# Time mixing in pairs of heads: the masked grams of the next pair formed in the tail of this one, the projections cut in six pieces between the level matmuls

## The chip, the cores and the metric

One core of a Trainium2 chip runs the whole kernel. Its engines are TensorE (PE; its weight loads are listed as PEld), VectorE (DVE), ScalarE (ACT), GpSimd (POOL) and SyncE (SP), which issues most DMAs. Each has its own queue and works through it in order; they wait for each other by semaphores. The metric is the device time of one execution in microseconds (us).

## The reference

Two transformer-like layers run on 128 context tokens and 128 latent tokens, which share the weights. All is fp32. The change touches only the time mixing of layer 0, a recurrence over the tokens in both directions, for 16 heads of 64 channels:

```python
def _rwkv7_step(S, inp):
    r, w, k, v, kk, a = inp
    sa = jnp.einsum('bdhij,bdhj->bdhi', S, -kk)
    S = S * w[..., None, :] + sa[..., None] * (kk * a)[..., None, :] + v[..., None] * k[..., None, :]
    return S, jnp.einsum('bdhij,bdhj->bdhi', S, r)
```

`r`, `k`, `v` are `(D, D)` projections of shifted inputs, `w` (decay) and `a` come from small two-step (LoRA) projections, `g` is a gate, and the result goes through a group norm per head, a bonus term `r . k . v` and an output projection. Behind it stand the SwiGLU of layer 0, the neighbourhood attention of layer 1 and its top-2 of 8 experts, which the change leaves as they are.

## The kernel before

The recurrence is solved in closed form over all 128 tokens of a sequence. The 16 heads are taken in eight pairs of two heads (`c` = 0 to 7; two heads, two sequences, so four problems `q`, and two directions `e`). Buffers of two pairs alternate (`p` = 0, 1). For each pair:

- `prep_project` (L545): r, k, v of a pair, three matmuls of eight 128-row chunks each, into PSUM banks 4 and 5. Every fp32 matmul shows as two records in the trace. `prep_gate` (L551) is the gate. ACT copies them out (`prep_rkv`, L1047 to L1053). They are made two pairs ahead (`ahead`).
- `prep_lora` (L564), `prep_norm` (L573), `prep_coef` (L579, L581), `prep_hat` (L589) prepare the next pair (`prep`): LoRA, key norms, bonus coefficients, transposes. ACT takes tanh, roots and exponentials (L1059 to L1078), DVE scans the decays (L1482) and normalises the keys (L1470, L1471), POOL forms the scaled factors (`prep_factors`, L1307 to L1319), DVE copies out bonus, v and hats (L1487, L1488, L1493).
- `gram` (L607): 128 x 128 products of those factors for each problem, twice (k = 1, 2) for each direction. DVE masks them out of PSUM (L1501) into `GB` and `GK`, and `pairs` (L1508 to L1512) starts the triangular inverse from them.
- `level_z`, `level_d` (L616, L625): five levels of doubling that grow the inverse of both 64-token halves. Each level is two blocks of eight 64 x 64 matmuls per direction; DVE masks (L1517), adds (L1526, L1524) and transposes (L1528) between them.
- `right_side` (L635, L637), `solve0`, `solve1`, `solve2` (L644, L651, L659): the solution, with a copy by ACT behind each (DVE adds the last, L1534).
- `outputs` (L673 to L685): the outputs and final state, which ACT copies out. The group norm of a pair (`gn_mean` L690, `gn_var` L694, on DVE L1539 to L1552) is done in the step of the next.

The order of all this is written out by hand: `mix_step` on each engine lists what is issued, and no planner moves it. `c` = 0 has a prologue. In PE's step the grams of the pair come first, then the LoRA of the next pair, the levels, the right side, and the three solves, each behind one of the three projections of the pair after next. The direction `e` uses PSUM banks 2e and 2e + 1 for grams, levels and solves alike.

## Time and profile before

| | us |
|---|---|
| three timed runs | 2109.75, 2120.48, 2122.73 (median 2120.48) |
| the profiled execution, its own time | 2112.75 |
| its span, first to last instruction | 2111.0 |
| time-mixing stage, first gram to output projection | 168.3 to 614.1 |
| PE, DVE, ACT, POOL busy over the whole span | 1840.9, 1400.8, 1091.5, 134.4 |

The page gives the mean granted clock of PE as 0.932 of full speed. A record of the timeline gives start and duration in us, engine, line, what it writes and reads, and how many instructions were merged; in brackets stands the idle time ahead of it and what ended that. The durations of matmuls are modelled at their end, so two records in a row overlap by a little: what one takes is best read from start to start.

### The profile page before, as it was taken

To read this page: it belongs to the slowest core of one execution; us is meant where nothing else is said; L and a number is where in the kernel's file an instruction comes from. 1 tells how busy PE (TensorE), PEld (TensorE's weight loads), DVE (VectorE), ACT (ScalarE), POOL (GpSimd) and SP (SyncE) were. 2 spreads that over 40 slices of the span, in tenths; PEclk is the share of its full clock that TensorE was granted. 3 is DMA by queue.
4 is the path that set the end of the run, shared out by engine and by line. 5 is a ranking of instruction groups with operands and counts; after the bars stand their busy time and mean duration, and the time that the engine had idled before them with its cause. 6 is when DMAs were issued, how large, how long until landed. Compare 5 with 4: busy or idle time off the path is not lost.

```text
span 2111.0 us, 32971 instructions
## 1 busy us (share of the span) xinstructions
PE 1840.9 (87%) x11460; PEld 1531.6 (73%) x11460; DVE 1400.8 (66%) x1978; ACT 1091.5 (52%) x1466; POOL 134.4 (6%) x208
## 2 busy tenths in 40 slices
PE   6657787888776999698984999999999999999997
PEld 5546666776665888577973787878787887878785
DVE  6824555444634555583215888888888898989897
ACT  6422222221112444482221877777778787878685
POOL 0022222122200000001100000000000000000000
PEclk9878889889787999899996999999999999999999
DMA  9501111101033555354422898888989897979890
GB/s 403 217 35 36 38 37 37 37 2 47 38 144 117 187 192 182 120 240 182 147 107 120 310 355 323 345 318 338 337 318 358 308 364 301 372 291 373 308 371 37
DMA packets 61371, 442.90 MB, mean 210 GB/s; under 512 B 7008, under 2 KB 8160, under 8 KB 10080
## 3 DMA queue, kind: packets, MB, share of 16 engines
q1 hardware_dynamic: 59184, 437.81, 54.2%
q10 hardware_dynamic: 1584, 2.79, 0.3%
q8 instruction: 62, 1.02, 0.2%
q0 software_dynamic: 512, 1.05, 0.1%
q14 instruction: 29, 0.24, 0.0%
HBM read 438.99 MB, written 2.62 MB: 209 GB/s over the span
## 4 chain that ended last, share of the span: by engine, by line
PE 79%; DVE 11%; issue 4%; ACT 3%; POOL 3%; DMA 1%; ACTq 0%; DVEq 0%; POOLq 0%
PE PS L768 30%; PE PS L794 16%; PE PS L492 4%; PE PS L545 4%; PE PS L837 3%; PE PS L524 3%; PE PS L927 2%; PE PS L625 2%; PE PS L947 2%; PE PS L842 1%; PE PS L504 1%; DVE W L1501 1%; PE PS L782 1%; PE PS L479 1%; DVE LO L1378 1%
## 5 line engine op out<-in xcount | busy, mean ns | idle before, releaser
L1378 DVE TENSOR_TENSOR LO<-W,HI 128x1024 fp32r<-128x1024 f32 x758 | 894.3, 1221 | 122.5 <-ACT HI L979 75.1
L979 ACT ACTIVATE HI<-W 128x1024 fp32r<-128x1024 f32 x758 | 785.8, 1062 | 156.1 <-PE PS L768 83.8
L768 PE MATMUL PS<-HI,XHI 128*128 128x512 f32 x968 | 391.2, 404 | 27.0 <-DVE XLO L1633 13.2
L768 PE MATMUL PS<-HI,XLO 128*128 128x512 f32 x968 | 379.2, 392 | 0.0
L768 PE MATMUL PS<-LO,XHI 128*128 128x512 f32 x968 | 292.9, 391 | 1.3 <-DVE LO L1378 0.6
L768 PEld LDWEIGHTS PS<-HI,XHI 128*128 128x128 f32 x968 | 182.3, 188 | 66.3 <-ACT HI L979 17.9
L768 PEld LDWEIGHTS PS<-LO,XHI 128*128 128x128 f32 x968 | 180.8, 188 | 45.8 <-DVE LO L1378 6.3
L768 PEld LDWEIGHTS PS<-HI,XLO 128*128 128x128 f32 x968 | 182.7, 189 | 34.9
L794 PE MATMUL PS<-HI,HHI 128*128 128x512 f32 x484 | 189.4, 391 | 1.5 <-ACT HHI L1161 1.5
L794 PE MATMUL PS<-HI,HLO 128*128 128x512 f32 x484 | 188.5, 389 | 0.0
L794 PE MATMUL PS<-LO,HHI 128*128 128x512 f32 x484 | 145.5, 389 | 0.0
L625 PE MATMUL PS<-W 64*64 64x64 f32 x1280 | 66.7, 279 | 52.9 <-DVE W L1517 52.8
L1161 ACT ACTIVATE HHI<-PS 128x256 fp32r<-128x256 f32 (+1 forms) x110 | 44.6, 406 | 120.8 <-PE PS L782 120.8
L1083 ACT ACTIVATE W<-PS 128x128 f32<-128x128 f32 x32 | 7.1, 274 | 193.2 <-PE PS L637 193.2
L794 PEld LDWEIGHTS PS<-HI,HHI 128*128 128x128 f32 x484 | 90.9, 188 | 20.2 <-ACT HHI L1161 1.7
L794 PEld LDWEIGHTS PS<-LO,HHI 128*128 128x128 f32 x484 | 90.9, 188 | 19.1
L794 PEld LDWEIGHTS PS<-HI,HLO 128*128 128x128 f32 x484 | 90.9, 188 | 18.6
L625 PEld LDWEIGHTS PS<-W 64*64 64x64 f32 x1280 | 61.5, 189 | 57.0 <-issue 57.0
L545 PE MATMUL PS<-B,W 128*128 128x256 f32 x384 | 92.4, 398 | 3.4 <-issue 3.4
L616 PE MATMUL PS<-W 64*64 64x64 f32 x1280 | 67.0, 273 | 26.3 <-DVE W L1501 25.6
L492 PE MATMUL PS<-HI,XHI 128*128 128x512 f32 x192 | 64.7, 419 | 27.7 <-DMA CON<-cons 16.3
L545 PEld LDWEIGHTS PS<-B,W 128*128 128x128 f32 x384 | 74.5, 198 | 15.1 <-issue 3.8
(280 smaller groups left out, 2269.3 us busy)
## 6 DMA issues: line engine op xcount, KB each, us to landing
W<-w_exp SPq DMA_DIRECT2D x298, 1024.0 KB, 5.5
W<-w_mod SPq DMA_DIRECT2D x48, 1024.0 KB, 8.9
W<-w_ffn SPq DMA_DIRECT2D x33, 1024.0 KB, 4.8
W<-w_rkv SPq DMA_DIRECT2D x8, 1792.0 KB, 7.3
W<-w_qkv SPq DMA_DIRECT2D x8, 1536.0 KB, 6.8
W<-w_o SPq DMA_DIRECT2D x1, 4096.0 KB, 19.3
W<-w_o SPq DMA_DIRECT2D x1, 3072.0 KB, 9.6
W<-w_qkv SPq DMA_DIRECT2D x8, 256.0 KB, 2.8
```

Source lines behind the costliest of these rows:

```text
L492: last = mm(PS[t % 2], XHI[:, 2 * n + k, 0:P], w[:, 512 * k:512 * k + 512], start=first and k == 0, stop=end and k == 1)
L524: last = mm(PS[2 + b % 2][:, TT * half:TT * half + TT], wo_tile(l, 2 * b + half, kc), src[:, kc], start=(kc == 0), stop=(kc == C - 1))
L545: last = mm(out, w[:, n, kc], B[n][:, kc], start=(kc == 0), stop=(kc == C - 1))
L616: last = mm(PS[2 * e][h, N * q:N * q + N], GB[e][h, q, 0, h], TN[e][h, q], start=True, stop=True)
L625: last = mm(PS[2 * e + 1][h, N * q:N * q + N], left[e][h, q], right[e][h, q], start=True, stop=True)
L768: last = mm(PS[2 * (s % 2) + g], x[:, 2 * n + k, T * g:T * g + T], w[:, 512 * k:512 * k + 512], start=(n == 0 and k == 0 and i == 0 and le ...
L794: last = mm(PS[4 + 2 * g + half], h[:, f, T * g:T * g + T], w[:, 512 * half:512 * half + 512], start=(s == 0 and f == 0 and i == 0 and len ...
L837: last = mm(PS[0][:, TT * n:TT * n + TT], w[:, n, kc], HT[:, kc], start=(kc == 0), stop=(kc == C - 1))
L927: last = mm(PS[1 + 2 * (c // 4)][:, P * (c % 4):P * (c % 4) + P], HN[:, g, P * c:P * c + P], SEL[:, g], start=(g == 0), stop=(g == G - 1))
L979: fn(HI[:, u % NBUF], raw_unit(phase, u), ACT.Copy).then_inc(hi_ready, 1)
L1161: fn(HHI[:, :, 0:width], PS[2 * (s % 2)][:, 0:2 * width].rearrange("p (f t) -> p f t", f=2), ACT.Copy).then_inc(hhi_ready, 1)
L1378: tt(LO[:, u % NBUF], raw_unit(phase, u), HI[:, u % NBUF].bitcast(F32), ALU.subtract)\
```

## The change

The grams of pair c + 1 are no longer made at the start of its own step but in the tail of step c, between and behind the solves, and DVE masks them and starts the inverse there. So `GB`, `GK` and `TR` exist for two pairs; they lie in an area that the split weights of the other phases use. All grams go through banks 2 and 3, one after the other; levels, right side and solves of direction e share bank e. The projections of pair c + 2 leave the solves and go, in six pieces of four chunks, behind the `level_z` of levels 2 to 5 and behind the `level_d` of levels 4 and 5. `prep_coef` and `prep_hat` stand behind all levels. On ACT both directions' right sides are copied together. On DVE `gn_centre` stands in level 1, the key floor and the decay scan behind it, the key reciprocal behind level 2, bonus and hat behind the levels, and `gn_tail` at the end of the step. Pair 0 gets its grams in the prologue.

```diff
@@ -148,6 +148,8 @@
         CON = sb("CON", NCON)
 
 
+        with nc.sbuf_tensor("MIX", [P, 2 * NBUF * UNIT + 2 * C * TT + 4 * TT], F32) as mix_area:
+            MIX = mix_area[:, :]
         HI = sb("HI", NBUF * UNIT, F32R).rearrange("p (n x) -> p n x", n=NBUF)
         LO = sb("LO", NBUF * UNIT, F32R).rearrange("p (n x) -> p n x", n=NBUF)
         XHI = sb("XHI", C * TT, F32R).rearrange("p (c t) -> p c t", c=C)
...
@@ -223,18 +225,19 @@
         PW = two(scratch(0, 2 * TT))
         PINV, PX = CUM, CUX
         HATT = LD.rearrange("p e t -> p (e t)").rearrange("p (n t) -> p n t", n=4)
-        GB = [scratch(0, 8 * P).rearrange("p (q k t) -> p q k t", q=4, k=2) for _ in range(2)]
-        GK = [scratch(0, 8 * P).rearrange("p (q k t) -> p q k t", q=4, k=2) for _ in range(2)]
+        GB, GK = [[[MIX[:, 1024 * (4 * n + 2 * b + e):1024 * (4 * n + 2 * b + e) + 1024]
+                    .rearrange("p (q k t) -> p q k t", q=4, k=2) for e in range(2)] for b in range(2)] for n in range(2)]
         TN = [scratch(0, 4 * N).rearrange("p (q t) -> p q t", q=4) for _ in range(2)]
-        TR = [scratch(0, 4 * N).rearrange("p (q t) -> p q t", q=4) for _ in range(2)]
...
+        RHS = [RHSA[:, e] for e in range(2)]
         U = [scratch(0, 4 * N).rearrange("p (q i) -> p q i", q=4) for _ in range(2)]
         WU = RHS
...
@@ -534,25 +538,26 @@
                 return (blk[:, 0:BLK].rearrange("p (n k m) -> p n k m", n=3, k=C),
                         blk[:, BLK:BLK + 384].rearrange("p (n m) -> p n m", n=3))
 
-            def prep_project(c, r, p, n):
+            def prep_project(c, r, p, n, half):
                 w, w2 = wblock(p)
-                if n == 0:
+                if n == 0 and half == 0:
                     pe.wait_ge(pair_full[p], 16 * (r + 1))
                     if not (isinstance(c, int) and c == 0):
                         pe.wait_ge(prep_act, 4 * (c - 1) + 2)
                 out = PS[4][:, TT * n:TT * n + TT] if n < 2 else PS[5][:, 0:TT]
-                for kc in range(C):
+                for kc in range(4 * half, 4 * half + 4):
...
-                    last.then_inc(prep_psum, 1)
+                if n == 1 and half == 1:
+                    last.then_inc(rkv_psum, 1)
...
@@ -595,88 +600,95 @@
                 return slice(N * hl, N * hl + N), slice(T * g, T * g + T)
 
             def gram(e, c, p, k):
-                if k == 1:
+                use = 4 * c + 2 * (k - 1) + e
+                if use == 0:
                     pe.wait_ge(prep_pool, 3 * c + 3)
-                    if not (isinstance(c, int) and c == 0):
-                        pe.wait_ge(chain_sbuf[e], CH * c)
                 else:
-                    pe.wait_ge(gram_sbuf[e], 2 * c + 1)
+                    pe.wait_ge(gram_sbuf, use)
+                    if k == 1 and e == 0:
+                        pe.wait_ge(prep_pool, 3 * c + 3)
                 for q in range(4):
                     rows, cs = heads(q)
-                    out = PS[2 * e + q // 2][:, 256 * (q % 2):256 * (q % 2) + 256].rearrange("p (k t) -> p k t", k=2)
+                    out = PS[2 + q // 2][:, 256 * (q % 2):256 * (q % 2) + 256].rearrange("p (k t) -> p k t", k=2)
                     last = mm(out, (BT if k == 1 else KT)[p][rows, e, cs], AR[p][e][rows, :, cs], start=True, stop=True)
-                last.then_inc(gram_psum[e], 1)
-
-            def level_z(e, c, n):
+                last.then_inc(gram_psum, 1)
+
...
                 pe.wait_ge(natural_sbuf[e], 5 * c + n)
-                if n == 1:
-                    pe.wait_ge(gram_sbuf[e], 2 * c + 2)
+                if n == 1 and c:
+                    pe.wait_ge(chain_sbuf[e], CH * c)
...
-                        last = mm(PS[2 * e][h, N * q:N * q + N], GB[e][h, q, 0, h], TN[e][h, q], start=True, stop=True)
+                        last = mm(PS[e][h, N * q:N * q + N], GB[p][e][h, q, 0, h], TN[e][h, q], start=True, stop=True)
                 last.then_inc(level_psum[e], 1)
...
-                        last = mm(PS[2 * e + 1][h, N * q:N * q + N], left[e][h, q], right[e][h, q],
+                        left, right = (tr, Z[e]) if n < 5 else (Z[e], tr)
+                        last = mm(PS[e][h, 256 + N * q:256 + N * q + N], left[h, q], right[h, q], start=True, stop=True)
+                last.then_inc(level_psum[e], 1)
+
+            def right_side(c, p):
+                for e in range(2):
+                    pe.wait_ge(turned_sbuf[e], 6 * c + 6)
+                pe.wait_ge(prep_dve, 6 * c + 5)
+                for e in range(2):
+                    for q in range(4):
+                        rows, _ = heads(q)
+                        at = 2 * N * e + N * (q % 2)
+                        mm(PS[q // 2][:, at:at + N], GK[p][e][:, q, 0], VN[p][:, q % 2, rows],
+                           start=True, stop=(q % 2 == 0))
+                    for q in (1, 3):
+                        rows, cs = heads(q)
+                        at = 2 * N * e + N
+                        last = mm(PS[q // 2][:, at:at + N], AR[p][e][rows, 0, cs], S0P[p][rows, e], start=False, stop=True)
+                last.then_inc(rhs_psum, 1)
+
+            def solve0(e, c, p):
+                pe.wait_ge(rhs_sbuf, c + 1)
+                for q in range(4):
+                    for h in HALVES:
+                        last = mm(PS[e][h, 256 + N * q:256 + N * q + N], TR[p][e][h, q], RHS[e][h, q],
                                   start=True, stop=True)
...
@@ -695,36 +707,36 @@
 
             def mix_step(c, p, prep, ahead, tail):
 
-                for e in range(2):
-                    gram(e, c, p, 1)
+                if prep is not None:
+                    prep_lora(*prep)
                 if tail:
                     gn_mean(c - 1)
-                if prep is not None:
-                    prep_lora(*prep)
-                for e in range(2):
-                    gram(e, c, p, 2)
-                if tail:
-                    gn_var(c - 1)
                 if prep is not None:
                     prep_norm(prep[0])
                 for n in range(1, 6):
                     for e in range(2):
-                        level_z(e, c, n)
+                        level_z(e, c, p, n)
+                    if ahead is not None and n > 1:
+                        prep_project(*ahead, (n - 2) // 2, n % 2)
+                    if tail and n == 2:
+                        gn_var(c - 1)
                     for e in range(2):
-                        level_d(e, c, n)
-                    if prep is not None and n == 4:
-                        prep_coef(prep[0])
-                if prep is not None:
-                    prep_hat(prep[0])
-                for e in range(2):
-                    right_side(e, c, p)
-                for n, f in enumerate((solve0, solve1, solve2)):
-                    if ahead is not None:
-                        prep_project(*ahead, n)
-                    for e in range(2):
-                        f(e, c)
+                        level_d(e, c, p, n)
+                    if ahead is not None and n > 3:
+                        prep_project(*ahead, 2, n - 4)
                 if ahead is not None:
                     prep_gate(ahead[2])
+                if prep is not None:
+                    prep_coef(prep[0])
+                    prep_hat(prep[0])
+                right_side(c, p)
+                for n, f in enumerate((solve0, solve1, solve2)):
+                    if prep is not None:
+                        gram(n % 2, prep[0], prep[1], 1 + n // 2)
+                    for e in range(2):
+                        f(e, c, p)
+                if prep is not None:
+                    gram(1, prep[0], prep[1], 2)
                 outputs(c, p)
 
             modulation(0)
@@ -744,6 +756,9 @@
             prep_coef(0)
             prep_hat(0)
             prep_rkv(1, 0, 1)
+            for k in range(1, 3):
+                for e in range(2):
+                    gram(e, 0, 0, k)
             mix_step(0, 0, (1, 1), (2, 1, 0), False)
             for i in range(2):
                 mix_step(2 * i + 1, 1, (2 * i + 2, 0), (2 * i + 3, i + 1, 1), True)
...
@@ -1077,22 +1092,21 @@
                 fn(PINV, CUM, ACT.Exp, scale=-1.0)
                 fn(PX, CUX, ACT.Exp).then_inc(prep_act, 1)
 
-            def right_side(e, c):
+            def right_side(c):
+                act.wait_ge(rhs_psum, c + 1)
+                for hl in range(2):
+                    last = fn(RHSA[:, :, 2 * hl:2 * hl + 2], PS[hl][:, 0:4 * N].rearrange("p (e g i) -> p e g i", e=2, g=2),
+                              ACT.Copy)
+                last.then_inc(rhs_sbuf, 1)
+
+            def solve0(e, c):
                 act.wait_ge(chain_psum[e], CH * c + 1)
-                for hl in range(2):
-                    last = fn(RHS[e][:, 2 * hl:2 * hl + 2],
-                              PS[2 * e + hl][:, 0:2 * N].rearrange("p (q i) -> p q i", q=2), ACT.Copy)
-                last.then_inc(chain_sbuf[e], 1)
-
-            def solve0(e, c):
+                fn(U[e], PS[e][:, 4 * N:8 * N].rearrange("p (q i) -> p q i", q=4), ACT.Copy).then_inc(chain_sbuf[e], 1)
+
+            def solve1(e, c):
+                then = HALVES[1 - e]
...
@@ -1108,6 +1122,8 @@
 
             def gn_root_(c):
                 act.wait_ge(gn_psum, 3 * c + 3)
+                if not (isinstance(c, int) and c == 0):
+                    act.wait_ge(z_ready, c)
                 fn(YR, PS[7][:, 0:TT], ACT.Sqrt, scale=1.0 / N, bias=BIASES[:, 1:2]).then_inc(gn_root, 1)
 
             def mix_step(c, prep, ahead, tail):
...
@@ -1554,31 +1574,32 @@
             def mix_step(c, p, prep, tail):
                 if prep is not None:
                     prep_params(prep[0], prep[2], prep[1])
-                for e in range(2):
-                    gram(e, c, 1)
-                if tail:
-                    gn_centre(c - 1)
-                for e in range(2):
-                    pairs(e, c)
-                    gram(e, c, 2)
-                if prep is not None:
-                    prep_floor(prep[0])
-                    prep_scan(prep[0])
                 for n in range(1, 6):
                     for e in range(2):
                         level_z(e, c, n)
+                    if tail and n == 1:
+                        gn_centre(c - 1)
                     for e in range(2):
-                        level_d(e, c, n)
+                        level_d(e, c, p, n)
                     if prep is not None and n == 1:
+                        prep_floor(prep[0])
+                        prep_scan(prep[0])
+                    if prep is not None and n == 2:
                         prep_unit(prep[0])
-                    if tail and n == 2:
-                        gn_tail(c - 1, 1 - p)
-                    if prep is not None and n == 4:
-                        prep_bonus(*prep[:2])
                 if prep is not None:
+                    prep_bonus(*prep[:2])
                     prep_hat(*prep[:2])
+                    gram(0, prep[0], 1 - p, 1)
+                    gram(1, prep[0], 1 - p, 1)
+                    pairs(0, prep[0], 1 - p)
+                    gram(0, prep[0], 1 - p, 2)
                 for e in range(2):
                     solve2(e, c)
+                if prep is not None:
+                    gram(1, prep[0], 1 - p, 2)
+                    pairs(1, prep[0], 1 - p)
+                if tail:
+                    gn_tail(c - 1, 1 - p)
 
             prep_params(0, 0, 0)
             prep_floor(0)
@@ -1586,6 +1607,12 @@
             prep_unit(0)
             prep_bonus(0, 0)
             prep_hat(0, 0)
+            gram(0, 0, 0, 1)
+            gram(1, 0, 0, 1)
+            pairs(0, 0, 0)
+            gram(0, 0, 0, 2)
+            gram(1, 0, 0, 2)
+            pairs(1, 0, 0)
             mix_step(0, 0, (1, 1, 0), False)
             with dve.Fori(0, 3) as i:
                 order.enter(i, STEPS_DVE_MIX)
```

On PE at the boundary of two steps stands before (PS4 to PS7 are banks; L685 is the end of `outputs`, L607 grams, L690 the group-norm mean, L564 the LoRA):

```order
L685 MATMUL PS7<-W 64x64
L607 MATMUL PS0<-W 128x256 [waits chain_sbuf0,prep_pool]
L607 MATMUL PS0<-W 128x256
L607 MATMUL PS1<-W 128x256 x2
L607 MATMUL PS2<-W 128x256 [waits chain_sbuf1,prep_pool]
L607 MATMUL PS2<-W 128x256
L607 MATMUL PS3<-W 128x256 x2
L690 MATMUL PS7<-extra,CON 128x256 [waits gn_sbuf]
L564 MATMUL PS4<-HID,W 128x256 [waits prep_act]
```

and in the changed kernel (L697 ends `outputs`, L569 is the LoRA, L702 the group-norm mean, L578 the key norm, L622 `level_z`):

```order
L697 MATMUL PS7<-W 64x64
L569 MATMUL PS4<-HID,W 128x256 [waits prep_act]
L569 MATMUL PS5<-HID,W 128x256
L569 MATMUL PS4<-HID,W 128x256
L569 MATMUL PS5<-HID,W 128x256
L702 MATMUL PS7<-W,CON 128x256 [waits gn_sbuf]
L578 MATMUL PS6<-W,CON 128x256 [waits prep_dve,prep_pool]
L622 MATMUL PS0<-W,MIX 64x64 [waits chain_sbuf0,natural_sbuf0]
```

The grams have left this place, and the LoRA, which waits for ACT, now follows the outputs directly.

On PE inside a level stands before (level 3; L616 `level_z`, L625 `level_d`):

```order
L616 MATMUL PS2<-W 64x64 [waits natural_sbuf1]
L616 MATMUL PS2<-W 64x64 x7
L625 MATMUL PS1<-W 64x64 [waits level_mask0,turned_sbuf0]
L625 MATMUL PS1<-W 64x64 x7
L625 MATMUL PS3<-W 64x64 [waits level_mask1,turned_sbuf1]
```

and in the changed kernel (level 4; L622, L632 the same two, L549 a piece of a projection):

```order
L622 MATMUL PS1<-W,MIX 64x64 [waits natural_sbuf1]
L622 MATMUL PS1<-W,MIX 64x64 x7
L549 MATMUL PS4<-B1,W 128x256 x4
L632 MATMUL PS0<-W 64x64 [waits level_mask0,turned_sbuf0]
L632 MATMUL PS0<-W 64x64 x7
L632 MATMUL PS1<-W 64x64 [waits level_mask1,turned_sbuf1]
L632 MATMUL PS1<-W 64x64 x7
L549 MATMUL PS5<-B2,W 128x256 x4
```

Half a projection of the pair after next now stands between the blocks of a level, and in levels 4 and 5 a second half behind them.

On DVE the end of a step is before (L1493 the hat copy, L1534 the last solve's add, L1461 and L1462 the first of the next step, L1501 the gram masks):

```order
L1493 COPY W<-PS6 128x512 [waits prep_psum]
...
L1534 TENSOR_TENSOR W<-W,PS0 64x256 [waits chain_psum0]
L1534 TENSOR_TENSOR extra<-extra,PS2 64x256 [waits chain_psum1]
...
L1461 TENSOR_SCALAR W<-W 128x128 [waits gn_psum]
```

and in the changed kernel (L1518 the gram masks, L1526 to L1530 the pairs group, L1553 the last solve's add, L1565 the first of the group-norm tail):

```order
L1518 TENSOR_TENSOR MIX<-PS2,CON 128x512 [waits gram_psum]
L1518 TENSOR_TENSOR MIX<-PS3,CON 128x512
...
L1553 TENSOR_TENSOR W<-W,PS0 64x256 [waits chain_psum0]
L1553 TENSOR_TENSOR W<-W,PS1 64x256 [waits chain_psum1]
L1518 TENSOR_TENSOR MIX<-PS2,CON 128x512 [waits gram_psum]
L1518 TENSOR_TENSOR MIX<-PS3,CON 128x512
L1526 TENSOR_TENSOR W<-MIX,CON 64x256 [waits gram_sbuf]
...
L1530 STREAM_TRANSPOSE W<-W 128x256 [waits turned_sbuf1]
L1565 RECIPROCAL W<-W 128x256 [waits gn_root]
```

Masks, pairs groups and the group-norm tail now stand around the last add, in a part of the step where DVE had little queued.

## Rows read from the trace of the kernel before

**Rows 1.** Table of windows: length, busy time (count) of PE, PEld, DVE, ACT, POOL, granted clock, DMA share, GB/s
```profile
285.20:343.50 58.30, 47.81 (x570) 41.11 (x568) 30.22 (x65) 13.18 (x27) 14.86 (x22) 0.82 0.10 34
...
168.30:620.00 451.70, 359.66 (x4442) 307.88 (x4442) 234.62 (x506) 96.49 (x200) 103.88 (x154) 0.85 0.10 36
```

**Rows 2.** Timeline of PE in pair 2, first half (start, duration in us, instruction, wait)
```profile
285.24 2.10 PE L607 MATMUL PS<-W 64*128 64x256 f32 x16
...
287.90 1.13 PE L564 MATMUL PS<-HID,W 64*128 64x256 f32 x8
...
292.74 0.68 PE L616 MATMUL PS<-W 64*64 64x64 f32 x16 [0.81 <-DVE W L1501]
...
297.53 1.98 PE L625 MATMUL PS<-W 64*64 64x64 f32 x32 [0.81 <-DVE W L1517]
...
303.02 1.97 PE L625 MATMUL PS<-W 64*64 64x64 f32 x32 [1.81 <-DVE W L1517]
...
311.14 1.97 PE L625 MATMUL PS<-W 64*64 64x64 f32 x32 [4.44 <-DVE W L1517]
...
318.54 1.15 PE L625 MATMUL PS<-W 64*64 64x64 f32 x32 [0.35 <-DVE W L1517]
```

**Rows 3.** The same timeline, second half of pair 2 and start of pair 3
```profile
320.11 0.56 PE L635 MATMUL PS<-W 128*128 128x64 f32 x4
...
323.81 3.72 PE L545 MATMUL PS<-B,W 128*128 128x256 f32 x16
...
327.46 1.15 PE L644 MATMUL PS<-W 64*64 64x64 f32 x32
...
336.73 0.96 PE L659 MATMUL PS<-W 64*64 64x64 f32 x16
...
338.41 0.40 PE L673 MATMUL PS<-W 128*64 128x128 f32 x2
...
343.51 2.10 PE L607 MATMUL PS<-W 64*128 64x256 f32 x16
```

**Rows 4.** Timeline of DVE in pair 2
```profile
289.63 0.85 DVE L1508 TENSOR_TENSOR W<-W,CON 64x256 f32<-64x256 f32 x2
...
291.35 1.25 DVE L1501 TENSOR_TENSOR W<-PS,CON 128x512 f32<-128x512 f32 x2
...
300.37 1.71 DVE L1470 RECIPROCAL W<-W 128x256 f32<-128x256 f32 x1
...
305.86 1.71 DVE L1546 RECIPROCAL extra<-extra 128x256 f32<-128x256 f32 x1
...
317.34 0.39 DVE L1487 TENSOR_TENSOR W<-PS,W 128x256 f32<-128x256 f32 x1
```

**Rows 5.** Table of windows, two of 2 us in pair 2
```profile
293.20:295.20 2.00, 0.22 (x8) 0.09 (x3) 1.93 (x5) 1.58 (x2) 0.00 (x0) 1.00 0.67 136
295.20:297.20 2.00, 1.12 (x16) 0.96 (x16) 2.00 (x7) 1.35 (x2) 0.05 (x1) 0.53 0.90 373
```

**Rows 6.** Timeline of ACT and POOL in pair 2, and ACT at the start of pair 3
```profile
289.09 0.84 ACT L1059 ACTIVATE W<-PS,W 128x256 f32<-128x256 f32 x2 [1.49 <-PE PS L564]
...
293.03 1.28 ACT L1111 ACT_TABLE_LOAD   x1
...
302.62 0.73 POOL L1307 TENSOR_TENSOR W<-W 128x256 f32<-128x256 f32 x1 [4.20 <-DVE W L1471]
...
315.14 0.61 POOL L1319 TENSOR_TENSOR W<-W 128x256 f32<-128x256 f32 x1
...
345.44 0.39 ACT L1053 ACTIVATE W<-PS 128x256 f32 x1
```

**Rows 7.** Timeline of PE at the starts of pairs 6 and 7 and behind pair 7
```profile
517.40 2.10 PE L607 MATMUL PS<-W 64*128 64x256 f32 x16
...
565.17 2.10 PE L607 MATMUL PS<-W 64*128 64x256 f32 x16
...
614.14 16.11 PE L524 MATMUL PS<-HT,W 128*128 128x256 f32 x61 [4.18 <-DVE HT L1552]
```

140 lines of the change are left out of this document (63 added, 77 removed).

## The prediction

> **What bounds the kernel now.** The change touches the time-mixing stage alone, so I read first the table of windows: the stage runs from 168.3 us to about 614 us, and TensorE (PE) is busy for 360 of its 452 us, twice anything else except VectorE's (DVE) 235 [rows 1]. Next the timeline of one pair in the middle. Pair 2 starts at 285.24, when the first gram matmul (L607) issues, and pair 3 at 343.51: a period of 58.3 us [rows 2, 3], of which PE is busy for 47.8 [rows 1]. So PE bounds the stage, but not by its work alone. Its waits all stand in the first half of the pair: the first level matmuls (L616) start 7.5 us into the pair, having waited for masked grams; the level-1 product (L625) starts 12.3 us in; then 1.81 us before level 2 and 4.44 us before level 3, where DVE is in a reciprocal of 1.71 us (L1470) and later in the group-norm tail that starts with another (L1546) [rows 2, 4]. In the second half PE waits for nothing: three projections stand between the solves. Last, the clock: PE does almost nothing from 293.2 to 295.2 at a granted clock of 1.00, and at 295.2 to 297.2 the grant is 0.53, which is a mix with the 1.2 GHz level [rows 5]. From there a block of 32 level matmuls takes 1.97 us, against 1.15 once 2.4 GHz is back [rows 2].
>
> **The change, part by part.** Nothing of the arithmetic is removed. I walk one pair of the new order, with t = 0 at the end of the outputs of the pair before, durations from rows, and 0.2 us for each hand-over between engines (DVE's mask ends at 292.60, the L616 that needs it starts at 292.74) [rows 2, 4].
>
> *Start of a pair.* The grams (2.0 us each time, L607) no longer stand first; the LoRA matmuls do (L564), and they wait for ScalarE (ACT) to copy out r, k, v and gate. That copy ends at 345.44 + 0.39, 2.3 us after outputs end at 343.5 [rows 3, 6]. Before, the grams covered this; now PE idles 2.5 us, a new wait. LoRA 1.0 (its record of 1.13 overlaps the next), the group-norm mean 0.6 (2.66 us from L607 to L564, less 2.0 for the grams), the key norm about 0.5: level 1 starts at 4.7 instead of 7.5, and its product at 6.0 instead of 12.3 [rows 2], because the grams are already masked.
>
> *Levels.* At 2.4 GHz the two L616 blocks take 1.1 us, so do the two L625 blocks [rows 2], and the masks (0.4 each) and the add and transpose (0.43 and 0.45) leave about 0.9 us of waits: 3.1 us a level. A half projection is 8 of the 16 records that take 3.65 us (323.81 to 327.46) [rows 3], 1.83 us. It goes in behind the second L616, where at most 0.3 us was idle, so each piece hides little and adds about 1.5. With the group-norm variance (0.5) in level 2, the key reciprocal in front of level 3, and a second piece in levels 4 and 5 the levels come to 3.1 + 5.1 + 5.1 + 6.1 + 5.8 and 0.5 for the gate: t = 30.4.
>
> *The chain beside it.* LoRA ends at 3.5; ACT's tanh group takes 3.9 (289.09 to 293.03) [rows 6] to 7.7; DVE scans behind level 1 and 1.3 us later; ACT's group-norm root waits for the variance at 11.5, then the key root, a table load and the exponentials to 15.8; DVE's reciprocal and product (2.1) end at 16.1; GpSimd's (POOL) factors take 13.1 (302.62 to 315.14 + 0.61) [rows 6] and end at 29.4. The coefficient matmul (L579), now behind the levels, needs them: it could start at 29.5 and PE arrives at 30.4. So this chain is covered, by 0.9 us only; a delay beyond that is paid in full in every pair.
>
> *Behind the levels.* Coefficient and transposes 0.85; then PE waits 1.0 for DVE's two short operations (0.39 for the first, L1487) with their hand-overs [rows 4], which stood under level 5 before; hat 0.5; right side 3.7 (320.11 to 323.81) [rows 3]: t = 36.5.
>
> *The tail.* It was 14.6 us (323.81 to 338.41, three projections and the solves) [rows 3]. Now four gram halves of 1.0 stand there with solves of 1.1, 0.9 and 0.9. All grams use the same two banks, so each waits for DVE's mask of the one before (1.25, and in front of the third mask also the pairs group, 1.72 from 289.63 to 291.35) [rows 4]: waits of 0.4, 0.7 and 1.1. Sum 9.1, t = 45.6; outputs 5.1 (338.41 to 343.51) [rows 3]: **50.7 us a pair against 58.3**, less 7.5. The group-norm tail moves behind the last pairs group on DVE; it ends about 2 us after the outputs, under the wait of 2.5 us, and nothing of PE waits for it but LoRA's tanh, which starts later still. If it grew by over 1 us it would delay the tanh, and with it the chain to POOL.
>
> *Ends of the stage.* Pairs 1 to 5 are of this form: 5 x 7.5 = 37.5 saved. Pair 0 has its grams masked ahead of it one after the other with little to cover them: 3 lost. Pair 6 has no projections and stands on the POOL chain: 29.5 + 0.9 + 1.0 + 0.5 + 3.7 + 9.1 + 5.1 = 49.8 against 47.8 (517.40 to 565.17) [rows 7]: 2 lost. Pair 7 has no grams left, about 4 us of them and the 6 us that its levels waited for masks and DVE: 10 to 12 saved. Together 44, with PE at 2.4 GHz throughout. The chain of the whole kernel runs through the stage's end: the output projection at 614.14 waited for DVE [rows 7], so the 44 would arrive whole.
>
> *The clock.* The old pair fell to 1.2 GHz at about 295, after PE had done one block of 0.68 us since 291.93 (292.74 less its wait) [rows 2, 5]. In the new pair the emptiest place is the start, 2.5 us idle and then 2.1 of work in 2.2: somewhat busier, so I cannot say that it never falls. A fall there makes levels 1 and 2 cost 0.8 us more per pair of blocks (four of them) and less what it covers, about 3.2 us. I take it in half of the pairs: 6 x 1.6 = 10 given back. Bounds: 0, and 31 (below).
> The Trainium skill speaks of this too ("TensorE: Matmul & The Clock Gate", the section on the HAM clock gate): an idle engine is throttled to half rate and activity releases it. Taken by itself this rule says that a stage with no long idle place stays at 2.4 GHz, which would be the 44 in full; what it asks against this change is the wait of 2.5 us at each start, which no trace of the kernel before shows in that surrounding.
>
> Sum: 44 - 10 = **34 us less**. The profiled execution took 2112.75 us, its span 2111.0, and the three timed runs lie at 2109.75, 2120.48 and 2122.73; from the mean of the four, 2116, this gives **2082 us**.
>
> **The rivals.**
> (a) The clock never falls: all 44, 2072 us. For it: of the 50.7 us PE would wait in about 8. Against: the start of the pair.
> (b) The clock falls at each start and stays low until the first whole projection is through. Levels 1 to 3 (six double blocks, 0.8 each) and a projection (3.65) at half rate, less the waits that they fill: 5.2 us a pair, 31 in all; 44 - 31 = 13 less, 2103 us. For it: before, the grant stayed low from 295 to 315 through blocks that were busy most of the time.
> (c) The ACT, DVE and POOL chain ends last. It has 0.9 us of cover. Each further 1 us costs 6 to 7 us over the pairs; 2 to 4 us late gives 8 to 22, so 2090 to 2104 us. For it: scan, root and reciprocal now queue behind level 1 and 2 on DVE, and I have placed them from single rows.
> (d) The other side: the 1.2 GHz level holds through all five levels, now with the projections inside them. Then 11.0 us of projections cost 11 more, ten double blocks 0.66 each 6.6 more, less 2.7 of waits: 14.9 a pair. That is 45 slower over the kernel, 2161 us; it decides as soon as about half of the level stretch runs low. Against it: with projections between, PE has hardly a gap there.
> (e) The change does not act as written, because the dependency chain through the levels on DVE sets the pair whatever PE does: 2116 us, no change. Against it: DVE is busy 30 of 58 us [rows 1].
>
> **How the numbers follow.** Forecast 0.56, (a) 0.14, (b) 0.12, (c) 0.10, (d) 0.04, (e) 0.04. One per cent, about what a measurement here can tell, is 21 us, so the border lies at 2099. Faster by over 1%: forecast, (a), most of (c) and a little of (b), 0.79. Within 1%: the rest of (b) and (c), and (e), 0.17. Slower: (d), 0.04. The range from 2066 to 2104 takes in the forecast, (a), (c) and half of (b).
>
> **What would show it.** In the new profile: a pair period near 51 us; PE idle 2.5 us before LoRA, released by ACT; first level matmul 4.7 us and coefficient 30 us after the outputs, released by PE's own queue and not by POOL; waits of about 0.4, 0.7 and 1.1 before the later grams, released by DVE; a pair 7 near 31 us; a granted clock in the stage above 0.93 where it was 0.85 [rows 1]. Wrong, if the coefficient waits for POOL, if the grant stays low through the projections, or if DVE is what ends most level waits by more than a microsecond.

## The result and the profile after

| | before | after |
|---|---|---|
| median, us (runs) | 2116.84 (4: 2109.75 to 2122.73) | 2064.90 (4: 2063.66 to 2065.97) |
| profiled execution, its span | 2112.75, 2111.0 | 2065.11, 2063.3 |
| mean granted clock, whole span | 0.932 | 0.950 |

The ratio is 0.9756, with a 95% interval of 0.9721 to 0.9791: 2.4% faster, 52 us by the medians and 48 by the two profiles, where 34 were forecast. The median lies 1 us below the range of 2066 to 2104.

First the page of the kernel after, its span and the first and clock lines of its parts 1 and 2:

```profile
span 2063.3 us, 32930 instructions
...
PE 1820.6 (88%) x11460; PEld 1498.0 (73%) x11460; DVE 1396.7 (68%) x1978; ACT 1088.1 (53%) x1450; POOL 132.5 (6%) x208
...
PEclk9877999998988999899987999999999999999999
```

Then the windows of the kernel after: the stage, one pair without a clock fall, the start of a pair in which the clock falls, and all that stands behind the stage.

```profile
168.30:565.90 397.60, 333.22 (x4428) 269.26 (x4427) 231.27 (x508) 93.29 (x184) 101.96 (x154) 0.94 0.10 36
229.57:278.40 48.83, 42.83 (x570) 34.52 (x568) 28.29 (x62) 12.72 (x25) 14.57 (x22) 1.00 0.11 41
281.60:285.00 3.40, 3.40 (x29) 2.40 (x28) 0.05 (x1) 2.97 (x6) 0.58 (x1) 0.51 0.00 0
285.00:288.40 3.40, 2.94 (x78) 2.52 (x76) 3.11 (x9) 2.14 (x3) 0.00 (x0) 0.99 0.46 105
565.90:2063.00 1497.10, 1378.73 (x6564) 1141.66 (x6564) 1068.58 (x1319) 921.92 (x1175) 15.83 (x28) 0.97 0.69 263
```

The same stretch of the kernel before, cut at its own end of the stage:

```profile
168.30:614.10 445.80, 353.80 (x4427) 303.19 (x4426) 234.62 (x506) 96.49 (x200) 103.88 (x154) 0.85 0.09 33
```

The stage went from 445.8 to 397.6 us, by 48.2, and what stands behind it kept its length (1497.1 us; before, 614.1 to 2111.0, 1496.9). DVE's, ACT's and POOL's work is nearly the same. PE is busy 20.6 us less on the same number of matmuls, with a grant of 0.94 instead of 0.85 and a faster right side (below), and idle 27.6 us less.

One pair of the new order in the timeline of PE (pair 1; the outputs of pair 0 end at 229.65, which is t = 0; L569 LoRA, L702 group-norm mean, L622 and L632 levels, L549 projection pieces, L584 coefficients, L594 hats, L643 and L648 right side, L613 grams):

```profile
229.37 0.28 PE L697 MATMUL PS<-W 128*64 128x64 f32 x2
231.66 1.14 PE L569 MATMUL PS<-HID,W 64*128 64x256 f32 x8 [2.01 <-ACT W L1068]
232.72 0.70 PE L702 MATMUL PS<-W,CON 128*128 128x256 f32 x2
...
233.87 1.15 PE L622 MATMUL PS<-W,MIX 64*64 64x64 f32 x32
235.17 1.15 PE L632 MATMUL PS<-W 64*64 64x64 f32 x32 [0.15 <-DVE W L1535]
...
238.06 1.99 PE L549 MATMUL PS<-B,W 128*128 128x256 f32 x8
...
245.40 1.15 PE L632 MATMUL PS<-W 64*64 64x64 f32 x32 [0.39 <-DVE W L1535]
...
259.26 0.59 PE L584 MATMUL PS<-W,CON 128*128 128x256 f32 x2
...
261.05 0.66 PE L594 MATMUL PS<-CON,W 128*128 128x128 f32 x4 [0.97 <-DVE W L1505]
261.54 1.00 PE L643 MATMUL PS<-W,MIX 128*128 128x64 f32 x8
262.48 0.44 PE L648 MATMUL PS<-W 64*128 64x64 f32 x4
...
264.15 1.13 PE L613 MATMUL PS<-W 64*128 64x256 f32 x8
...
266.67 1.14 PE L613 MATMUL PS<-W 64*128 64x256 f32 x8 [0.30 <-DVE MIX L1518]
...
272.08 1.14 PE L613 MATMUL PS<-W 64*128 64x256 f32 x8 [0.84 <-DVE MIX L1518]
...
278.06 0.28 PE L697 MATMUL PS<-W 128*64 128x64 f32 x2
```

Outputs end again at 278.34: 48.7 us for the pair (49.0 from LoRA to LoRA), where the old one took 58.3 [rows 2, 3]. LoRA starts 2.0 us into the pair, level 1 at 4.2, its product at 5.5 (12.3 before [rows 2]), the coefficients at 29.6. The later gram blocks wait 0.30 to 0.84 us for DVE to mask the one before out of their banks. The levels hold no wait above 0.4 us; the old ones had 1.81 and 4.44 [rows 2].

Waits of PE by what ended them, over the stage, in the kernel before:

```profile
PE PS L625 <- DVE W L1517: 52.8, 30, 4.9
PE PS L616 <- DVE W L1501: 25.6, 16, 2.2
PE PS L579 <- POOL W L1319: 5.2, 1, 5.2
```

and in the kernel after:

```profile
PE PS L613 <- DVE MIX L1518: 15.5, 23, 1.4
PE PS L569 <- ACT W L1068: 13.2, 6, 2.3
PE PS L632 <- DVE W L1535: 7.2, 16, 2.3
PE PS L594 <- DVE W L1505: 6.7, 7, 1.0
PE PS L584 <- POOL W L1335: 4.5, 1, 4.5
```

(Columns: us in total, times, the longest.) The level products waited 52.8 us for DVE and now wait 7.2; the first level waited 25.6 us for masked grams and now waits for none. What came in their place is smaller: grams 15.5 (of it 4.2 ahead of pair 0), LoRA 13.2, hats 6.7.

### The profile page after: what moved, and what is told of

Read it like the earlier page. It is cut to its first block, busy times and chain, and to the rows that moved or that the text cites. A ratio compares the mean times of both kernels' runs of the same rounds, so it can differ in the third digit from the quotient of the medians.

```text
span 2063.3 us, 32930 instructions
## 1 busy us (share of the span) xinstructions
PE 1820.6 (88%) x11460; PEld 1498.0 (73%) x11460; DVE 1396.7 (68%) x1978; ACT 1088.1 (53%) x1450; POOL 132.5 (6%) x208
## 4 chain that ended last, share of the span: by engine, by line
PE 82%; DVE 10%; ACT 3%; issue 3%; POOL 1%; DMA 1%; ACTq 0%; DVEq 0%; POOLq 0%
PE PS L783 31%; PE PS L809 16%; PE PS L496 5%; PE PS L549 4%; PE PS L852 3%; PE PS L528 3%; PE PS L942 2%; PE PS L962 2%; PE PS L613 1%; PE PS L857 1%; PE PS L508 1%; PE PS L622 1%; DVE MIX L1518 1%; PE PS L797 1%; PE PS L632 1%
## 5 line engine op out<-in xcount | busy, mean ns | idle before, releaser
L783 PE MATMUL PS<-HI,XHI 128*128 128x512 f32 x968 | 391.2, 404 | 27.2 <-DVE XLO L1660 13.2
L809 PEld LDWEIGHTS PS<-HI,HHI 128*128 128x128 f32 x484 | 90.9, 188 | 20.2 <-ACT HHI L1178 1.7
L809 PEld LDWEIGHTS PS<-LO,HHI 128*128 128x128 f32 x484 | 90.9, 188 | 19.1
L809 PEld LDWEIGHTS PS<-HI,HLO 128*128 128x128 f32 x484 | 90.9, 188 | 18.6
L549 PE MATMUL PS<-B,W 128*128 128x256 f32 x384 | 97.2, 402 | 3.4 <-issue 3.4
L1098 ACT ACTIVATE W<-PS 128x256 f32<-128x256 f32 x16 | 5.3, 381 | 158.0 <-PE PS L648 158.0
L549 PEld LDWEIGHTS PS<-B,W 128*128 128x128 f32 x384 | 73.0, 198 | 15.5 <-issue 3.8
L1518 DVE TENSOR_TENSOR MIX<-PS,CON 128x512 f32<-128x512 f32 x64 | 40.9, 681 | 50.9 <-PE PS L613 50.9
L1641 DVE TENSOR_TENSOR HLO<-PS,HHI 128x256 fp32r<-128x256 f32 (+1 forms) x110 | 49.5, 450 | 35.2 <-ACT HHI L1178 25.1
L1431 DVE RECIPROCAL RMS<-RMS 128x256 f32<-128x256 f32 x4 | 7.0, 1753 | 95.6 <-ACT RMS L1027 95.6
```

Source lines behind the costliest of these rows:

```text
L549: last = mm(out, w[:, n, kc], B[n][:, kc], start=(kc == 0), stop=(kc == C - 1))
L783: last = mm(PS[2 * (s % 2) + g], x[:, 2 * n + k, T * g:T * g + T], w[:, 512 * k:512 * k + 512], start=(n == 0 and k == 0 and i == 0 and le ...
L809: last = mm(PS[4 + 2 * g + half], h[:, f, T * g:T * g + T], w[:, 512 * half:512 * half + 512], start=(s == 0 and f == 0 and i == 0 and len ...
L1518: last = tt(dst[:, 2 * hl:2 * hl + 2].rearrange("p q k t -> p q (k t)"), PS[2 + hl].rearrange("p (q x) -> p q x", q=2), m, ALU.mult)
L1641: tt(HLO[:, :, 0:width], PS[2 * (s % 2)][:, 0:2 * width].rearrange("p (f t) -> p f t", f=2), HHI[:, :, 0:width].bitcast(F32), ALU.subtract ...
```

## The experiments

Each is an edit of one of the two kernels. e1 to e4, e5 to e8 and e9 to e11 ran in three groups, each on another chip and each beside runs of the kernel before, whose medians there were 2112.15, 2118.05 and 2106.91; a ratio is to those runs beside it. So medians are compared within a group, and across groups the ratios.

"First gram" is where the time-mixing stage starts in the profiled execution and "stage" is the time from there to the output projection; "pairs 1 to 5" is the time from the second LoRA to the seventh, "pairs 6, 7" from there to the output projection; "low" is the time of the stage at the 1.2 GHz level, worked out from the mean granted clock of short windows. All are in us.

| run | median (runs) | ratio, 95% interval | first gram | stage | pairs 1 to 5 | pairs 6, 7 | low |
|---|---|---|---|---|---|---|---|
| before | 2116.84 (4) | | 168.3 | 445.8 | 290.4 | 94.1 | 131 |
| after | 2064.90 (4) | 0.9756, 0.9721 to 0.9791 | 168.3 | 397.6 | 249.1 | 85.1 | 49 |
| e1_before_rhs | 2104.86 (10) | 0.9970, 0.9955 to 0.9984 | 167.4 | 438.6 | 286.3 | 92.0 | 120 |
| e2_after_oldrhs | 2085.21 (4) | 0.9887, 0.9863 to 0.9910 | 165.0 | 421.0 | 259.8 | 94.9 | 85 |
| e3_before_projlevel | 2087.70 (4) | 0.9887, 0.9858 to 0.9917 | 167.6 | 430.7 | 278.5 | 95.5 | 102 |
| e4_after_projsolve | 2152.73 (4) | 1.0201, 1.0179 to 1.0223 | 168.6 | 486.0 | 322.6 | 87.2 | 178 |
| e5_filler | 2063.91 (5) | 0.9745, 0.9721 to 0.9769 | 167.7 | 400.1 | 247.3 | 89.5 | 55 |
| e6_rkv | 2065.07 (5) | 0.9747, 0.9722 to 0.9771 | 167.1 | 400.0 | 247.0 | 91.8 | 65 |
| e7_hat | 2059.88 (5) | 0.9736, 0.9712 to 0.9760 | 165.1 | 395.0 | 247.0 | 86.1 | 52 |
| e8_outorder | 2065.08 (5) | 0.9751, 0.9728 to 0.9773 | 168.2 | 398.9 | 245.8 | 90.1 | 57 |
| e9_all | 2053.85 (6) | 0.9724, 0.9694 to 0.9753 | 167.1 | 389.2 | 238.3 | 90.9 | 51 |
| e10_endfill | 2060.22 (6) | 0.9760, 0.9731 to 0.9789 | 167.0 | 397.1 | 249.1 | 84.6 | 38 |
| e11_all_endfill | 2042.18 (6) | 0.9686, 0.9655 to 0.9717 | 164.5 | 383.4 | 237.6 | 86.3 | 27 |

The first gram stands at 164.5 to 168.6 us, though PE's work ahead of it is the same in all of them. The reason is the clock ahead of the stage; here is one window of 20 us with the same work of PE, first in the kernel after, then in e7_hat:

```profile
100.00:120.00 20.00, 16.60 (x57) 13.50 (x56) 14.51 (x38) 2.44 (x4) 0.00 (x0) 0.76 0.00 1
100.00:120.00 20.00, 16.60 (x73) 14.13 (x72) 13.83 (x36) 2.43 (x4) 0.00 (x0) 0.95 0.01 1
```

So up to 4 us between two whole executions can come from ahead of the stage, and none of that belongs to an edit.

### The right side's order

I had carried the right side over at 3.7 us, and the new pair shows 2.6 (261.54 to 264.15). The diff had also regrouped its matmuls. e1_before_rhs gives the kernel before that order alone (lines that repeat `rows` and `out` are left out):

```diff
-                    mm_last = mm(out, GK[e][:, q, 0], VN[p][:, q % 2, rows], start=True, stop=(q % 2 == 0))
-                    if q % 2:
-                        mm_last = mm(out, AR[p][e][rows, 0, cs], S0P[p][rows, e], start=False, stop=True)
+                    mm(out, GK[e][:, q, 0], VN[p][:, q % 2, rows], start=True, stop=(q % 2 == 0))
+                for q in (1, 3):
...
+                    mm_last = mm(out, AR[p][e][rows, 0, cs], S0P[p][rows, e], start=False, stop=True)
```

> The kernel before, with one thing of the change: in each direction's right side all four GK matmuls are issued first and then the two of 64 rows, instead of two and one, twice. Nothing else moves. Theory (a turn between 128-row and 64-row matmuls costs time of its own, which is why a pair's right side fell from 3.7 to 2.6 us): the right side takes 2.7 us or less, the pair period falls by about 1 us, the kernel by 7 to 9 us. Rival (the right side got shorter because its operands or banks moved): 3.7 us stays, no change of the time.

Timeline of PE in e1_before_rhs, the right side of one pair (L635 the 128-row matmuls, L639 the 64-row ones, L545 the projection behind them):

```profile
317.02 1.00 PE L635 MATMUL PS<-W 128*128 128x64 f32 x8
317.96 0.44 PE L639 MATMUL PS<-W 64*128 64x64 f32 x4
318.33 1.10 PE L635 MATMUL PS<-W 128*128 128x64 f32 x8
319.36 0.44 PE L639 MATMUL PS<-W 64*128 64x64 f32 x4
...
```

The projection follows at 319.73: 2.7 us against 3.7 [rows 3], with the same matmuls. The stage is 7.3 us shorter and so are the medians, where eight right sides by 1.0 would give 8. e2_after_oldrhs is the reverse, the old order put into the new kernel (the output operand is written `...`):

```diff
                     for q in range(4):
                         last = mm(..., GK[p][e][:, q, 0], VN[p][:, q % 2, rows], start=True, stop=(q % 2 == 0))
+                        if q % 2:
+                            last = mm(..., AR[p][e][rows, 0, cs], S0P[p][rows, e], start=False, stop=True)
-                    for q in (1, 3):
-                        last = mm(..., AR[p][e][rows, 0, cs], S0P[p][rows, e], start=False, stop=True)
```

> The changed kernel with the old order inside the right side: two GK matmuls, then one of 64 rows, twice per direction; its banks, buffers and the common copy stay as changed. Theory (the order is the cause): the right side takes 3.7 us again, a pair 50.1 instead of 49.0, the kernel 7 to 9 us more than the changed one, about 2073 us. Rival (banks or buffers): 2065 us, no difference.

Timeline of PE and windows of e2_after_oldrhs:

```profile
262.19 0.66 PE L594 MATMUL PS<-CON,W 128*128 128x128 f32 x4 [0.97 <-DVE W L1504]
262.68 0.56 PE L643 MATMUL PS<-W,MIX 128*128 128x64 f32 x4
263.17 0.43 PE L646 MATMUL PS<-W 64*128 64x64 f32 x2
263.53 0.66 PE L643 MATMUL PS<-W,MIX 128*128 128x64 f32 x4
```

```profile
262.60:266.00 3.40, 3.40 (x25) 2.95 (x23) 0.69 (x1) 0.00 (x0) 0.00 (x0) 0.99 0.02 5
266.00:269.40 3.40, 3.40 (x29) 2.51 (x30) 0.79 (x2) 0.66 (x2) 0.00 (x0) 0.51 0.00 0
```

The grouped order has two turns from 128-row to 64-row matmuls and back where the old one has four, and saves 1.0 us: 0.5 for a turn there and back. The right side is back at 3.7. But the stage grew by 23.4 us, not by 8 x 1.0, and the kernel was expected 7 to 9 us longer and is 20 longer by the medians (2085.21 against 2064.90) and 28 by the ratios: 36 us more were run at the 1.2 GHz level. In the two windows PE is busy throughout, and the grant falls at the end of the slow right side; but a wait of 0.97 us, that of the hats for DVE, ends at 262.19, just ahead of them. The kernel after has the same wait there and no fall behind it. So the order is worth 7 to 8 us by itself, and in the new kernel some 15 more, by the stage, by way of the clock.

### One part of the change without the other

e3_before_projlevel leaves the grams where they were and puts the six pieces between the level matmuls; e4_after_projsolve has the grams in the tail and the projections at the solves. All else of the change (the place of the coefficients and hats, the banks, the orders of ACT and DVE, the grouped right side) is absent in e3 and present in e4:

```diff
# e3_before_projlevel, against before
                         level_z(e, c, n)
+                    if ahead is not None and n > 1:
+                        prep_project(*ahead, (n - 2) // 2, n % 2)
...
-                        prep_project(*ahead, n)
# e4_after_projsolve, against after
-                        prep_project(*ahead, (n - 2) // 2, n % 2)
...
                         gram(n % 2, prep[0], prep[1], 1 + n // 2)
+                        for half in range(2):
+                            prep_project(*ahead, n, half)
```

> The kernel before with the six projection pieces alone moved between the level matmuls; the grams stay at the start of their own pair, in four banks, and the solves stand bare. Theory (the pieces fill the waits for DVE in levels 2 and 3 and keep the clock up, which pays for most of the gain): about 20 us less than before, 2092 to 2100 us, a pair of 55 to 56 us. Rival (the gain needs the grams moved, since waits of the first level and solves without cover give all back): within 8 us of before.

> The changed kernel with the projections back between the solves, whole; the grams stay in the tail of the pair before. Theory (the coefficient matmul behind the levels then stands on the chain ACT, DVE, POOL, since the levels end some 10 us before POOL's factors, and the solves hold both projections and grams): slower than before, a pair of 60 to 62 us, 2130 to 2142 us, and PE waits for POOL 8 us or more in each pair. Rival (moving the grams is the part that gains by itself): 2090 us or less.

Waits of PE over the stage in e3_before_projlevel:

```profile
PE PS L627 <- DVE W L1521: 33.1, 18, 4.9
PE PS L618 <- DVE W L1505: 25.5, 16, 2.2
```

and in e4_after_projsolve, with the coefficient matmul of one pair:

```profile
PE PS L584 <- POOL W L1334: 35.9, 7, 5.6
PE PS L632 <- DVE W L1534: 27.1, 29, 2.3
```

```profile
337.93 1.22 PE L584 MATMUL PS<-W,CON 128*128 128x256 f32 x2 [5.10 <-POOL W L1334]
```

In e3 the pieces fill 19.7 of the 52.8 us that the level products waited, and the stage is 15.1 us shorter; the wait for masked grams is whole, 25.5. This profile is of the longest of e3's four runs (2095.15, where the others took 2082.84 to 2091.66), and by the medians e3 is 24.5 us below the kernel before, where about 20 were expected. In e4 that wait is gone, and PE reaches the coefficients about 5 us before POOL has the factors, in every pair. This is rival (c), made real by taking its cover away. The levels, short blocks with waits of DVE between them, then run low for long: 178 us of the stage against 131. So the stage is 40.2 us longer than before. The direction was expected; the wait was put at 8 us or more and the kernel at 2130 to 2142, so the low clock cost more than I had allowed for.

The parts do not add up. By the medians of this group, moving the projections into the levels is worth 24.5 us with the grams at the start (2112.15 to 2087.70), and some 88 with the grams in the tail (the stages of e4 and of the kernel after, 486.0 and 397.6). The grams in the tail, with all that moves along with them, cost 47.9 us as long as the projections stand at the solves (e1 to e4, 2104.86 to 2152.73; the stage 47.5). With the projections in the levels they save, but how much depends on the right side: with its old order 2.5 us by the medians (e3 to e2, 2087.70 to 2085.21) or 9.7 by the two profiled stages, e3's being of its longest run. With the grouped order no run holds that kernel without the grams moved. If the order were worth e1's 7.3 in e3 too, the stage of 430.7 would be 423.4, and the kernel after is 26 below that. This is an estimate; between the two, 53 us less are run at the low level.

### The start of the pair, and small edits

The longest regular waits of the kernel after are LoRA's for ACT (2.0 to 2.3 us) and the hats' for DVE (0.97). e5_filler puts four matmuls whose result nobody reads into the first; e6_rkv lets ACT copy r, k, v before the outputs; e7_hat puts the hats behind the right side; e8_outorder regroups the outputs by height, as the right side was.

```diff
# e5_filler
+                if prep is not None and tail:
+                    pe.wait_ge(prep_dve, 6 * c + 6)
+                    for k in range(4):
+                        mm(PS[6][:, TT:2 * TT], HEADS, B[0][:, k], start=True, stop=True)
                 if prep is not None:
                     prep_lora(*prep)
# e6_rkv, on ACT
-                outputs(c)
                 if ahead is not None:
                     prep_rkv(ahead)
+                outputs(c)
# e7_hat
                     prep_coef(prep[0])
+                right_side(c, p)
+                if prep is not None:
                     prep_hat(prep[0])
-                right_side(c, p)
# e8_outorder: the two S0P matmuls of q = 1 and 3 stand behind the other matmuls of all four q
```

> The changed kernel with four extra matmuls of 128 x 256 per pair (pairs 1 to 6), ahead of the LoRA, in the 2.0 to 2.3 us in which PE waits for ACT; their result is never read. They take 1.8 us, so they delay nothing. Theory (the granted clock falls at the start of a pair because PE waits there, and each fall costs 1.5 us, 50.5 against 49.0): no fall in pairs 1 to 5, all of them 49.0, 4 to 7 us less than the changed kernel, though PE does more. Rival (the difference of 1.5 us is something else, or the falls don't come from this wait): no change, or slower by what the matmuls overrun.

> The changed kernel with ACT's copy of r, k, v and gate ahead of its copy of the outputs and state, since the projections are complete long before; PE's order is as it was. Theory (the LoRA waits 2.0 to 2.3 us at the start of each pair for this copy, and that wait ends last there): the wait goes, the group-norm mean and the key norm wait some 0.5 us instead, 1.5 us less in a pair, 7 to 11 us less over the kernel. Rival (the chain ACT, DVE, POOL ends last): POOL starts earlier too, so only if PE waits for POOL at the coefficient would nothing be gained.

> The changed kernel with the four hat transposes behind the right side instead of ahead of it, so that DVE's bonus and v copies are under the right side. Theory (the wait of 0.97 us that ends with DVE's copy, L1505, is paid in full): 1.0 us less in each of pairs 0 to 6, 7 us less, and more if the denser end of the pair keeps the clock up. Rival (DVE's hat copy, which now comes later, delays the first gram mask by as much): no change, and the wait ahead of the second gram grows by 0.7 us.

> The changed kernel with the outputs' four matmuls of 64 rows at the end of the output group instead of two and two in its middle. Theory (a turn between 128-row and 64-row matmuls costs 0.15 to 0.3 us, as the right side showed): one block of them less, 0.3 to 0.5 us less in a pair, 2 to 4 us over the kernel. Rival (the shorter right side came from something special to it): no change.

Windows of e5_filler in the tail of pair 2:

```profile
308.20:311.60 3.40, 2.43 (x22) 2.10 (x21) 1.44 (x3) 0.00 (x0) 0.00 (x0) 1.00 0.01 2
311.60:315.00 3.40, 3.40 (x18) 2.67 (x17) 0.00 (x0) 0.66 (x2) 0.00 (x0) 0.51 0.00 0
315.00:318.40 3.40, 3.40 (x40) 2.98 (x40) 1.29 (x2) 0.77 (x2) 0.00 (x0) 0.50 0.02 5
```

With the start of the pair filled, no grant falls there in pairs 1 to 5 (in the kernel after it does in three of them, as at 281.6 in the window above), and the pair at full clock stays 49.0: the wait was the cause of those falls, though not each such wait brings one. But one fall came behind the hats' wait instead and lasted 6.8 us, and that pair took 51.7. Pairs 1 to 5 together are 1.8 us shorter, and pairs 6 and 7 are 4.4 us longer, with more time at the low level (31 us against 21), so that nothing is left of the 4 to 7 us that were expected. e8 goes the same way (3.3 us less, then 5.0 more), and so does e6 (2.1 less in pair 0 and 2.1 in pairs 1 to 5, then 6.7 more). Why the grant falls more often at the end of the stage in these runs is not shown.

e6 removes LoRA's wait and was expected to give 7 to 11 us. Its pair 1 takes 46.9 us, 2.1 less than 49.0, but the four pairs behind it take 49.1 to 51.6. The row of its new wait:

```profile
PE PS L578 <- POOL W L1305: 12.9, 6, 3.1
```

The longest of them, 3.1, stands in pair 0 and did so before the edit. The other five, 1.9 to 2.1 us each, are new: in pairs 2 to 6 the key norm behind LoRA waits for POOL, 9.8 us in place of the 13.2 that LoRA waited. Pair 1 alone has no such wait. e7 removes the hats' wait; every one of its pairs 1 to 5 has a fall at its start and takes 49.1 to 49.5, and its stage is the shortest of the four, 2.5 us below that of the kernel after, of an expected 7; another 3.2 us of its shorter execution lie ahead of the stage. e8 takes 0.37 us off a pair at full clock (48.65), as expected. All four ratios lie within the interval of the kernel after: none of these edits is told from it by its time.

e9_all joins the edits of e6, e7 and e8. e10_endfill fills the ends of the stage with unread matmuls, in the levels of pair 6, ahead of its coefficients, and in the waits of the last group norm; e11_all_endfill has both. (In pair 6 e10 and e11 have two `filler` matmuls in each of levels 2 to 5 and five ahead of the coefficients; the excerpt shows the end of the stage.)

```diff
+            def filler(n):
+                for _ in range(n):
+                    mm(PS[4][:, 0:TT], HEADS, CON[:, 0:TT], start=True, stop=True)
...
+            filler(1)
             gn_mean(7)
+            filler(2)
             gn_var(7)
+            filler(9)
             pe.wait_ge(z_ready, C)
```

> The changed kernel with the three edits of the runs before together: r, k, v copied ahead of the outputs, hats behind the right side, 64-row matmuls of the outputs in one block. Theory (each is worth its part in a pair at full clock: 2.1, 1.0 and 0.35 us, and what a run gives besides depends on where the granted clock falls, 1.5 us and more for each fall): undisturbed pairs of 45.5 to 46 us where they were 49.0, the stage 10 to 20 us shorter, 2045 to 2057 us. Rival (falls of the clock take back what the pairs gain, as in the runs of each edit alone): 2058 to 2066 us with more than 65 us of low grant in the stage.

> The changed kernel with extra matmuls of 128 x 256 on constants, never read, where PE waits in the last two pairs: two in each of levels 2 to 5 of pair 6 and five ahead of its coefficient matmul, which waits 4.5 us for POOL, then one, two and nine in the waits of the last group norm. Theory (in pair 6 and behind pair 7 the low grant, 20 of the stage's 50 us of it, comes from waits, and the first output projection pays for it too, 17.0 us for 64 records): the grant stays high there, PE does 12 us more work and the kernel takes 5 to 12 us less. Rival (the falls there don't come from idle time, or the extra work is in the way): no change or up to 5 us slower.

> Both together: the three edits and the extra matmuls at the end. Theory (they add up, since one acts in the pairs and the other behind them): 5 to 12 us less than the kernel with the three edits alone. Rival (the falls only move): the same time as that kernel within 3 us.

Pairs 1 and 4 of e9_all, as windows from LoRA to LoRA, both at full clock:

```profile
227.19:272.79 45.60, 42.52 (x570) 34.49 (x568) 27.86 (x61) 12.60 (x25) 14.53 (x22) 1.00 0.12 44
369.77:417.52 47.75, 42.52 (x571) 34.48 (x569) 29.45 (x66) 12.60 (x25) 14.55 (x22) 1.00 0.12 41
```

The expected 45.5 to 46 us is met by pair 1 alone. From pair 2 on the key norm waits 2.2 to 2.4 us for POOL, as in e6, and three of those four pairs take 47.75 to 48.0 without a fall. Against 49.0 that is e7's 1.0 and e8's 0.37 and no more: the wait for POOL takes e6's part back from pair 2 on.

The end of the stage in the kernel after:

```profile
565.86 17.00 PE L528 MATMUL PS<-HT,W 128*128 128x256 f32 x64 [4.18 <-DVE HT L1572]
```

and in e10_endfill:

```profile
564.10 14.08 PE L528 MATMUL PS<-HT,W 128*128 128x256 f32 x64 [0.29 <-DVE HT L1585]
```

The filler cannot shorten DVE's chain, and DVE still ends last; but the output projection starts at full clock, 14.1 us instead of 17.0 (15.7 to 17.1 in all runs without the fillers at the end, 14.08 in both with them). The profile of e10 is 4.8 us shorter by its span (2058.5): 1.3 ahead of the stage, 0.5 in it and 3.0 behind it, in this row. The fillers in pair 6 gave next to nothing in time, although 11 us less were low. The ratio of e10, 0.9760, is not told from 0.9756, and e9's 0.9724 is not either, since its interval reaches to 0.9753. e11 is at 0.9686, with an interval that ends at 0.9717, just below that of the kernel after (from 0.9721). Measured side by side, e11's median is 11.7 us below e9's and 18.0 below e10's. By the profiles of e9 and e11 that is 2.6 us ahead of the stage, which no edit made, 5.8 in it, most of that in pairs 6 and 7 (90.9 to 86.3), and 3.2 behind it; so some 8 us, within the 5 to 12 that were expected, can be the fillers'. e11 is the fastest version here: 3.1% below the kernel before; without unread matmuls it is e9, 2.8%.

## Why the prediction was wrong

The direction, the mechanism and the order of events were right; the size was not, and the median fell 1 us out of the range. By its steps, with t = 0 at the end of the outputs:

| step | forecast | measured |
|---|---|---|
| LoRA, level 1, its product start at | 2.5, 4.7, 6.0 | 2.0, 4.2, 5.5 |
| coefficients start, POOL's factors end | 30.4, 29.4 | 29.6, 28.2 |
| wait for DVE ahead of the hats | 1.0 | 0.97 |
| right side | 3.7 | 2.6 |
| tail, its waits | 9.1; 0.4, 0.7, 1.1 | 9.0; 0.30, 0.51, 0.84 |
| pair at full clock | 50.7 | 49.0 |
| pair 0; pairs 1 to 5 at full clock; pairs 6 and 7 | 3 lost; 37.5 saved; 8 to 10 saved | 2.0 lost; 45.8 saved; 9.0 saved |
| given back by the clock in pairs 1 to 5 | 8 of the 10 | 4.5 |

The last two rows are worked out from the starts of LoRA. The second one is at 229.66 before and 231.66 after, both in a stage that starts at 168.3; the next five periods sum to 290.4 and 249.1, 41.3 saved with three clock falls of 1.5 us each (periods of 50.5 instead of 49.0, and 50.2 in pair 5, which takes 48.7 without a fall in e5), so 45.8 without them; the rest of the stage is 94.1 and 85.1.

**The step that failed** is "right side 3.7", which I carried over "3.7 (320.11 to 323.81)" as unchanged work at an unchanged price. The diff in the new `right_side` put all four 128-row matmuls ahead of the two 64-row ones, and I read it as the same matmuls. It measured 2.6. e1 and e2 show what the order was worth: 1.0 to 1.1 us a pair, 7 to 9 in all, by itself, and 23 in the stage once the clock is counted in the new kernel. e2_after_oldrhs is the kernel that the prediction priced, with the right side at 3.7: it took 2085.21 (by its ratio 2093) where 2082 was forecast, well inside the range. The prediction had no row of a regrouped block, but the line of the diff should have been a term with bounds.

**The clock** was the second term that came out otherwise, and it hangs on the first. "I take it in half of the pairs: 6 x 1.6 = 10 given back" had the place right for the kernel after (the start, as e5 shows) and the number of falls (three of five), but a fall there lasts only about 3.4 us (grant 0.51 at 281.6 to 285.0, 0.99 from 285.0) and costs 1.5 us, not 3.2. I had taken levels 1 and 2 whole at the low level, from the old kernel, where it stayed low for up to 20 us. In e2, whose pair at full clock would be 1.1 us longer than 49.0, pairs 1 to 5 take 259.8 us: some 9 of them are given back to the clock, about the 8 that were forecast, but part of its falls stand behind the right side and not at the start. So the size of the clock's term was near for the slow right side and too large for the grouped one.

The two terms together give 34 + 8.8 + 5.5 = 48.3; the stage shortened by 48.2. That they meet so closely is in part luck: without its right sides the stage saved some 3 us more than forecast in pairs 1 to 5 and some 2 less in pairs 6 and 7, whose low clock is not counted in the 5.5. A small slip stands in the border of 2099: it is 1% below 2120.48, while the forecast counts from 2116, 1% below which is 2095.

Rival (a), no falls, at 2072, came nearest by its number and was wrong as a case: there are falls. With the right side corrected it would be 2063, so the two errors cannot be told by the total alone. Rival (b), low until the first whole projection, did not occur in pairs 1 to 5. Rival (c) did not in pairs 1 to 5: in pair 1 POOL ends 1.4 us before PE gets there, and the coefficients are released by PE's own queue; in pair 6, where no projections stand in the levels, they waited 4.5 us for POOL, as I had assumed there. e4 shows that (c) was real and near. Rival (d), PE at 1.2 GHz through all levels, did not occur: pairs 1 to 5 ran 10 us low in all. e4 comes closest to it, 178 us low without the projections in the levels, which is what had been said against (d). Rival (e) is out: the level waits on DVE were filled.

The Trainium skill ("TensorE: Matmul & The Clock Gate", the section on the HAM clock gate) says that an idle engine is throttled and activity releases it. The trace agrees at the start of pair 2, where the fall at 281.6 follows 2.34 us without work, though pairs 1 and 3 start after 2.01 and 2.31 without a fall. e2's fall at 266.0 has 3.8 us of full occupation ahead of it and a wait of 0.97 ahead of that; whether the rule covers it no run here shows.

**What stays open.** Why the grant falls in stretches in which PE is nearly always busy, and why pairs 6 and 7 of e5, e6, e8 and e9 run low for some 10 us more than those of the kernel after. The stretches hold many short matmuls (64 columns, or half the rows), and filling idle places moved the falls more than it removed them. No run here varied the size of the matmuls at equal occupation, so this is an observation and not a cause. That it is the turn of heights that costs, and not an adding matmul directly behind the one that it adds to, is argued and not shown: the outputs' 128-row matmuls add four in a row into the same columns at 0.22 us each (273.42 to 274.08 in the kernel after), but no run separates the two.

## What to carry to other kernels

A matmul block that waits for nobody (here projections for the pair after next) belongs where another engine's short operations stand between dependent blocks, but before work is moved forward, count what it covered: the grams in the tail cost 48 us with the projections at the solves, since POOL's chain then ends last, and save 2.5 us or more with the projections in the levels. Read each regrouped loop of a diff as a change of its own, and keep matmuls of equal height together.

Where an engine's clock depends on its activity, split each execution into what stands ahead of the edit, every unit, and what stands behind, before an edit is given a gain or a loss. One unit is not enough: pair 1 of e9 took 45.6 us and the pairs behind it 47.75 and more. Three edits, none of which could be told from no change by its ratio, are together 11 us shorter by the span (2063.3 to 2051.9), of which 8.3 lie in the stage, and even together their ratio is not told from that of the kernel after.

## What the runs showed of the hardware

- The same 12 matmuls of a right side took 3.7 us when 128-row and 64-row ones alternated and 2.6 to 2.7 grouped (before, e1); the same regrouping of the outputs gave 0.37 us a pair (e8). For each turn there and back that went, this is 0.4 to 0.5 us.
- A clock fall in pairs 1 to 5 of the kernel after lasts 3.4 us (grant 0.51 in one window, 0.99 in the next) and costs 1.5 us of the period. They stand behind waits of 2.3 us at the start of a pair and are gone when the wait is filled (e5); in e2 and e5 falls came 2 to 4 us behind a wait of only 0.97 us.
- The output projection behind a wait of 4.2 us took 15.7 to 17.1 us, and 14.1 when that wait was filled with unread matmuls (e10, e11).
- The runs of one kernel lie in groups some 5 us apart: e7 ran four times at 2059.3 to 2060.0 and once at 2065.35, the kernel before near 2106.7, 2112.5, 2118 and 2122. Between profiles up to 4 us of this lie ahead of the stage, with a grant of 0.76 or 0.95 over the same work. An effect under 5 us has to be looked for within a trace.
